# Attention logits: two 256-key tiles side by side, with masks and a fill in matching order

## The reference

```python
# att1: 16 heads of 64
logits = jnp.einsum('bqhd,bqkhd->bhqk', qb, kg).astype(f32) * att_scale
logits = jnp.where(valid, logits, -jnp.inf)
p = jax.nn.softmax(logits, axis=-1).astype(vg.dtype)
return jnp.einsum('bhqk,bqkhd->bqhd', p, vg)
# att2: 8 heads of 64, a bias by distance, three dilated patterns merged
scores = einsum(q, k) * (ATT_HEAD_DIM ** -0.5) + alibi
scores = jnp.where(valid, scores, -jnp.inf)
```

## Time and profile before

| | us |
|---|---|
| median of 3 runs | 1945.39 |
| lowest, highest | 1945.06, 1946.08 |
| the profiled execution | 1944.47 |
| its span, first to last instruction | 1942.4 |
| att1 from the first logits to the last values | 758.7 to 842.5 |
| att2 likewise | 1452.4 to 1503.4 |

### The profile page before, as it was taken

The page is one execution under the profiler, slowest core; times in us unless marked ns, Lnnn a source line. Parts: engine busy times, 40 slices in busy tenths (PEclk is TensorE's granted clock), DMA queues, the critical chain, the costliest instruction groups (busy, mean ns, idle before and its releaser), DMA issues.

```text
span 1942.4 us, 26536 instructions
## 1 busy us (share of the span) xinstructions
PE 1890.6 (97%) x9610; PEld 1528.6 (79%) x9610; DVE 774.6 (40%) x1382; ACT 807.5 (42%) x1179; POOL 856.8 (44%) x421
## 2 busy tenths in 40 slices
PE   6999999999999999999999999999998999999997
PEld 4878788888887786578888888877885888888886
DVE  7852232222016999825222200456477062222103
ACT  4663344443125444835344421446246254344211
POOL 6544354444433243844444444434335444444441
PEclk9999999999999999999999999999999999999998
DMA  2143242333232232022323232332320323323331
GB/s 107 27 148 98 74 127 87 98 96 99 96 97 87 66 98 76 1 67 89 105 86 105 90 103 95 101 98 76 131 76 1 98 90 94 104 90 98 98 97 44
DMA packets 51832, 170.81 MB, mean 88 GB/s; under 512 B 6696, under 2 KB 11560, under 8 KB 51248
## 3 DMA queue, kind: packets, MB, share of 16 engines
q1 hardware_dynamic: 50320, 164.99, 27.4%
q10 hardware_dynamic: 1440, 4.83, 0.7%
HBM read 165.34 MB, written 2.10 MB: 86 GB/s over the span
## 4 chain that ended last, share of the span: by engine, by line
PE 91%; DVE 5%; ACT 1%; DMA 1%; DVEq 1%; issue 1%; SPq 0%; ACTq 0%
PE ps L238 24%; PE ps L240 24%; PE ps L239 24%; PE ps L1590 3%; PE ps L1592 3%; PE ps L1591 3%; PE ps L1289 2%; PE ps L1303 1%; PE ps L1311 1%; PE ps L820 1%; DVE h_lo L1212 1%; DVE xT L1135 1%; DMA s_gains<-in_s_gain 1%; PE ps L1629 1%; PE ps L1609 0%
## 5 line engine op out<-in xcount | busy, mean ns | idle before, releaser
L228 POOL TENSOR_TENSOR w_lo<-raw,w_hi 128x1024 fp32r<-128x1024 f32 x296 | 712.8, 2417 | 972.9 <-ACT w_hi L221 972.9
L238 PE MATMUL ps<-h_hi,w_hi 128*128 128x512 f32 (+1 forms) x1456 | 570.6, 392 | 4.2 <-DVE h_lo L1212 2.8
L240 PE MATMUL ps<-h_hi,w_lo 128*128 128x512 f32 (+1 forms) x1456 | 566.8, 389 | 0.0
L239 PE MATMUL ps<-h_lo,w_hi 128*128 128x512 f32 (+1 forms) x1456 | 566.6, 389 | 0.0
L221 ACT ACTIVATE w_hi<-raw 128x1024 fp32r<-128x1024 f32 x296 | 311.5, 1057 | 487.5 <-PE ps L240 436.8
L238 PEld LDWEIGHTS ps<-h_hi,w_hi 128*128 128x128 f32 (+1 forms) x1456 | 272.2, 187 | 64.5 <-issue 7.5
L240 PEld LDWEIGHTS ps<-h_hi,w_lo 128*128 128x128 f32 (+1 forms) x1456 | 272.1, 187 | 58.3
L239 PEld LDWEIGHTS ps<-h_lo,w_hi 128*128 128x128 f32 (+1 forms) x1456 | 272.3, 187 | 57.7 <-issue 0.5
L238 PE MATMUL ps<-hid_hi,w_hi 128*128 (+1 forms) x528 | 205.4, 389 | 0.0
L239 PE MATMUL ps<-hid_lo,w_hi 128*128 (+1 forms) x528 | 205.4, 389 | 0.0
L240 PE MATMUL ps<-hid_hi,w_lo 128*128 (+1 forms) x528 | 205.4, 389 | 0.0
(11 more groups left out here) (379 smaller groups left out, 2096.2 us busy)
## 6 DMA issues: line engine op xcount, KB each, us to landing
raw<-in_w_gu SPq DMA_DIRECT2D x132, 512.0 KB, 3.5
raw<-in_w_down SPq DMA_DIRECT2D x66, 512.0 KB, 3.5
raw<-in_w_mix SPq DMA_DIRECT2D x33, 512.0 KB, 3.5
raw<-in_w_dsa SPq DMA_DIRECT2D x29, 512.0 KB, 3.5
raw<-in_w_glu SPq DMA_DIRECT2D x16, 512.0 KB, 3.8
raw<-in_w_out SPq DMA_DIRECT2D x12, 512.0 KB, 3.5
raw<-in_w_o SPq DMA_DIRECT2D x8, 512.0 KB, 3.5
s_x<-in_xs SPq DMA_DIRECT2D x1, 2048.0 KB, 11.2
```

Source lines behind the costliest of these rows:

```text
L228: pool.tensor_tensor(w_lo[slot][:], raw[slot][:], w_hi[slot][:].bitcast(F32), ALU.subtract)\
L238: pe.matmul(o, wh, ah, start=start, stop=False)
L239: pe.matmul(o, wh, al, start=False, stop=False)
L240: return pe.matmul(o, wl, ah, start=False, stop=stop)
```

## The change

(0,1) keeps bank 4 alone. (1,1) moves to columns 0 to 255 of bank 0, in which (0,3), the 512-key tile of head 0, stood until its mask had read it. TensorE now computes (1,0), (0,0), (0,1), (1,1) in the second half of a pair, so that the two 256-key tiles follow one another in different banks. The wait of (1,1) for (0,1) goes; in its place (1,1) waits for the mask of (0,3) of its own pair. VectorE and ScalarE take (1,1) before (0,1). A table `FULL_FOR` gives each mask the number of logits that it waits for: 1 for (0,3), 2 for (1,3), 5 for (1,2) and (1,0), 6 for (0,2) and (0,0), 7 for (0,1), 8 for (1,1). By `BANK_READ` the (0,3) of the next pair now waits for seven masks of the pair before, where it waited for one. Ahead of the loop (1,1) of pair 0 moves behind the fill.

```diff
-        LOGITS = [(0, 3), (1, 3), (0, 2), (1, 2), (0, 1), (1, 0), (1, 1), (0, 0)]
+        LOGITS = [(0, 3), (1, 3), (0, 2), (1, 2), (1, 0), (0, 0), (0, 1), (1, 1)]
         L_AT = {(0, 3): (0, 0), (1, 3): (1, 0), (0, 2): (2, 0), (0, 0): (2, 3 * P), (1, 2): (3, 0), (1, 0): (3, 3 * P),
-                (0, 1): (4, 0), (1, 1): (4, 2 * P)}
-        MASKS = [(0, 3), (1, 3), (1, 2), (1, 0), (0, 2), (0, 0), (0, 1), (1, 1)]
+                (0, 1): (4, 0), (1, 1): (0, 0)}
+        MASKS = [(0, 3), (1, 3), (1, 2), (1, 0), (0, 2), (0, 0), (1, 1), (0, 1)]
...
+        FULL_FOR = {which: LOGITS.index(which) + 1 if which == (0, 3) else BANK_FULL[L_AT[which][0]] for which in LOGITS}
...
-                if j:
+                if (s, tb) == (1, 1):
+                    pe.wait_ge(a.masked, 8 * j + NTH_MASK[(0, 3)])
+                elif j:
                     pe.wait_ge(a.masked, 8 * (j - 1) + BANK_READ[bank])
-                if (s, tb) == (1, 1):
-                    pe.wait_ge(a.L_ready, 8 * j + LOGITS.index((0, 1)) + 1)
...
-            logits(0, range(4, 8))
+            logits(0, range(4, 7))
             if fill is not None:
                 fill(0)
+            logits(0, range(7, 8))
             logits(1, range(4))
...
-                    dve.wait_ge(a.L_ready, 8 * j + BANK_FULL[bank])
+                    dve.wait_ge(a.L_ready, 8 * j + FULL_FOR[s, tb])
```

## The result

With the change the median is 1949.75 us (1947.26 to 1951.32, 13 runs) against 1945.15 (1944.08 to 1946.80, 13 runs): ratio 1.0023, 95% interval 1.0016 to 1.0030. That is 4.6 us slower. It is inside the forecast range of 1944.5 to 1950.0, but only 0.25 us from its end, near the price of rival (c) and above the forecast's own case of +0.2 to +3.5. The profiled execution took 1949.35 us with a span of 1947.1, so the two spans differ by 4.7 us.

A forecast was written before the change was run, and what follows sets the result against it. TensorE was taken as the bound, at 91% of the chain, with three engines close behind. Att1's +0.3 and att2's +1.3 gave +1.6 us: 1946.1 profiled, 1947.0 as median, range 1944.5 to 1950.0.

The forecast's parts named there:

- rival (c): Layer entries: broken-up TensorE work keeps the clock at 1.2 GHz for further stretches; some +4.8 us, 1950.2; chance 16%.
- the forecast's own case: Whole kernel: small loop gains, larger losses at both layer entries; +0.2 to +3.5 us, chance 61%.
- The logits block: Four logits tiles of a pair: 0.84 us instead of 1.44, with the two 256-key tiles overlapping; 0.60 less for TensorE.
- The loop: Steady pairs of both layers: of the 0.60 us only 0.16 a pair comes through, period 7.93 us.
- The new waits inside the loop: Steady pairs: (1,1) and the next pair's (0,3) wait for masks that end well before; cost nothing.
- 3.07 + 0.73 + 4.02 + 0.11: Loop from one pair's values start (V) to the next: copy, low part, end of evacuation, values; 7.93 us.
- The entry of att1: Way into the first attention layer: waits for seventh masks make the first pair's values 1.1 us late; layer net +0.3.
- rival (c)'s third stretch: Logits of pair 1, now between idle times: another stretch at 1.2 GHz, 1.6 us lost on full work.
- The entry of att2: Way into the second attention layer: (1,1) behind the fill and mask waits make values 1.5 us late; layer net +1.3.
- (a): All eight loops: the whole 0.60 us comes through and both entries cost nothing; -4.8 us, 1940.6; chance 5%.
- (d): Logits block: the two 256-key tiles don't overlap, 0.42 us more, hidden in idle time; about 1947.5 us; chance 5%.
- (b): Loops gain as forecast or a little more, entries hidden by a high clock; -1.0 to 0, about 1944.9 us; chance 13%.

The follow-up runs named there:

- e9: Changed kernel with the old placing of (1,1) in pairs 0 and 1 of both layers, and 512-key logits one turn earlier; 1944.46 us, 0.9997 of the kernel before.
- e5: Changed kernel with ScalarE's evacuation of turn 3 ahead of the two small scales, nothing else; 1946.06 us, 1.0001 of the kernel before.
- e6: Changed kernel with matmuls of constants, results unused, in TensorE's pauses at the layer entries; 1945.64 us, 1.0002 of the kernel before.
- e3: Changed kernel with old placing in pairs 0 and 1 of both layers, and ScalarE's turn 3 evacuation before two small scales; 1941.86 us, 0.9978 of the kernel before.

## Why the prediction was right or wrong

The total lies in the range, but by luck: the forecast's own sum was +1.6, and the time came near the upper end because two terms above all were too good, one in the loop and one at the entry of att1. Neither the median nor its place in the range speaks for the working; the terms, one by one, do.

**The logits block**: right, 0.86 measured and 0.84 forecast. The two 256-key tiles overlap.

**The new waits inside the loop**: right. Ahead of the block and ahead of the first logits there is no idle time in the timeline of a pair.

**The loop, wrong**: the step that failed is the sum 3.07 + 0.73 + 4.02 + 0.11, in "From the low part to the end of the evacuation". In the timeline after, from V at 801.91, the steps are 3.07 to the copy of turn 0, 0.71 to the low part, 4.20 to the end of the evacuation and 0.10 to the values: 8.08, not 7.93. The 4.02 was too short by the 0.17 that the first mask waited for TensorE. The prediction let the first mask of pair j+2 follow the low part. That mask has a second releaser, the (0,3) logits of its own pair, which come behind the values, turn 0 and turn 1. By this releaser, again from 801.91: values 2.30, two turns 1.03, (0,3) in two passes 1.13 (e9's row for the 512-key pair has that length), 0.14 to the mask at 806.51; 2.81 from there to ScalarE's evacuation at 809.32, 0.57 and 0.10 to the values. Sum 8.08. Before, the same logits start at 794.89 and so ended at 796.02, and the mask started 0.14 behind them at 796.16. The row of the mask has no bracket, since the low part ahead of it on VectorE ended at nearly the same moment, and I took VectorE's own order for the only limit. TensorE's work, 8.08 us a pair, and this chain, 8.08 us, were equal; cutting the first left the second. Price of the error: six loops by 0.15 us, 0.9.

The Trainium skill, "TensorEngine Tiling (Array Packing)", section PSUM Bottleneck, says that the copy out of PSUM may become the bottleneck after a speedup by tiles. The runs agree (e5 against the changed kernel: 7.50 for 8.08), and with more than I gave it: the chain that ends in this copy took all 0.58 us, not three quarters.

**The entry of att1, right in kind, under half its size**: 1.1 forecast, 2.56 measured. The wait itself was exact: the seventh mask of pair 0 ends 12.64 after the first logits in both kernels (771.32 before, 771.03 after). The step that failed is "from a logits start to the mask of its first tile takes 1.16", a row at full clock. From the mask's end it took 773.20 - 771.03 = 2.17, not 0.10 + 1.16 = 1.26, since the clock had already fallen (0.50 from 771.00 on). So the first mask of pair 1 came 1.85 late instead of 0.94, the scales 1.6 instead of 0.4, the logits of pair 2 2.93 instead of 1.7. From there to V the shorter block gave back 0.37 (2.93 - 2.56) of the 0.6 that I had. The price: 1.5 us. This is rival (c)'s third stretch, "where the logits of pair 1 now stand between idle times".

**The entry of att2, right**: on the common scale the logits of pair 1 came 0.74 late (0.8 forecast), those of pair 2 started at 20.98 (21.06 forecast), turn 2 came 2.4 late (2.45 at the low clock), the scales took 7.18 for 6.95. V came 1.93 late, at the end of my 0.75 to 1.9; I took 1.5. The price: 0.4.

**The sum**: 1.5 + 0.9 + 0.4 = 2.8 us are missing of the +1.6, which gives 4.4, the two layers together. Rival (c) had the total nearly right and for att1 the mechanism: its low stretch at pair 1 was seen, by e6 most of the loss is the clock; and the clock had not risen by the end of pair 2's logits (0.50 to 783.09), the sign that it named. But part of what came near its 4.8 is the loop, of which it said nothing. Rivals (a) and (d) fell with the loop and the block; (b) with the entries.

## What to carry to other kernels

When an edit shortens one engine's part of a loop, list every releaser of every step of the remaining chain and add up each path; a releaser that ends at nearly the same moment as the work ahead in the engine's own order (here 0.14 us before the mask started) is a limit of equal rank, though no bracket names it. Here it took one reordering on another engine (here two scales behind an evacuation) to turn a gain of nothing into 0.58 us a pair. A buffer shared in steady state is paid where the pipeline is short: put the old placing in the first pairs (e3). And price a new pause ahead of TensorE's work with that work at half the clock, not only with the pause.

## What the runs showed of the hardware

The low clock can be worth more than the wait that brings it: about 3.5 us against 1 us here, by V0 in the profiled executions of the changed kernel and e6, and work that ran in 1.77 us at 1.00 took 3.36 at 0.50.

Tiles on different rows of TensorE overlap pass by pass. Narrow windows of the changed kernel, TensorE, inside the block from 807.96:

```profile
807.96 0.49 PE L1290 MATMUL ps<-kT,qT 64*128 64x128 f32 x4
...
808.29 0.60 PE L1290 MATMUL ps<-kT,qT 64*128 64x256 f32 x4
```

Four passes of 128 columns take 0.49 us and four of 256 take 0.60, side by side. Before, the second pass of one 256-key tile started at 797.94 and the first of the other only 0.52 later, at 798.46.

Eight scales of VectorE take 2.46 us in att1 and 7.18 in att2, beside GpSimd's copies and subtractions. The groups by form of the changed kernel, with busy time and mean ns of one, first from 1467.3 to 1474.7 (GpSimd busy), then from 776.0 to 778.6 (GpSimd idle):

```profile
L2275 POOL TENSOR_TENSOR mix_lo<-convT,mix_hi 128x512 fp32r<-128x512 f32 x4 | 5.2, 1317 | 0.2 <-issue 0.2
L1447 DVE TENSOR_SCALAR pr<-pr,den 128x512 f32<-128x512 f32 x2 | 2.2, 1112 | 0.1
```
```profile
L1447 DVE TENSOR_SCALAR pr<-pr,den 128x512 f32<-128x512 f32 x2 | 1.0, 483 | 0.1
```

The same instruction takes 2.3 times as long. That GpSimd's work is the cause is argued from these rows and was not tried.
